# A decoder block's expert layer: the last quarter of the experts computed densely on TensorE beside the gathers of the rest

## What is computed

```python
q = (h @ w_peer_q).reshape(b, s, 8, 2, 128)
sc = jnp.einsum('bshcd,hckd->bshck', q, peer_keys)
s1, i1 = lax.top_k(sc[..., 0, :], 16)
s2, i2 = lax.top_k(sc[..., 1, :], 16)
cand_s = s1[..., :, None] + s2[..., None, :]
cand_i = i1[..., :, None] * 128 + i2[..., None, :]
top_s, pos = lax.top_k(cand_s, 16)        # of the 256 pairs
eid = take_along_axis(cand_i, pos)
gate = softmax(top_s)
act = gelu(einsum('bthkd,btd->bthk', peer_u[eid], h))
out = x + einsum('bthk,bthkd->btd', gate * act, peer_v[eid])
```

## Time and profile before

| | |
|---|---|
| median of 3 runs | 2677.69 us |
| the profiled execution, its time | 2674.36 us |
| its span (first to last instruction) | 2672.7 us |
| mean granted TensorE clock | 0.811 of full |
| busy: TensorE, VectorE, ScalarE, GpSimd | 1696.7, 1703.4, 780.6, 710.3 us |
| bytes read from HBM | 771 MB, of which the gathers' queue 549 MB |

### The profile page before, as it was taken

How to read it: one execution, slowest core, us unless ns; L and a number is a source line. 1 busy time by engine, 2 the same in 40 slices (tenths; PEclk the granted TensorE clock), 3 DMA queues, 4 the chain that set the end, 5 groups by cost and what they waited for, 6 DMA issues and landing times.

```text
span 2672.7 us, 29348 instructions
## 1 busy us (share of the span) xinstructions
PE 1696.7 (63%) x9753; PEld 1263.9 (47%) x9753; DVE 1703.4 (64%) x2813; ACT 780.6 (29%) x1250; POOL 710.3 (27%) x617
## 2 busy tenths in 40 slices
PE   7899999999999999999850223223223222322335
PEld 6798888888888988878850000000000000000001
DVE  5888637766766766775787566665666665665530
ACT  4456445545554554545330000000000000000000
POOL 1000001001001001040125554435544435444332
PEclk9799999999999999999985665665666666656667
DMA  5244555665556556565778999999999999999998
GB/s 181 85 150 134 177 178 182 196 188 181 169 191 196 164 189 197 164 227 182 259 260 342 420 420 420 420 420 419 417 419 418 414 421 415 420 416 420 420 380 317
DMA packets 210987, 774.25 MB, mean 290 GB/s; under 512 B 18920, under 2 KB 54112, under 8 KB 143456
## 3 DMA queue, kind: packets, MB, share of 16 engines
q0 software_dynamic: 75584, 549.49, 50.2%
q1 hardware_dynamic: 134832, 223.61, 26.4%
q10 hardware_dynamic: 496, 0.23, 0.0%
HBM read 771.09 MB, written 2.16 MB: 289 GB/s over the span
## 4 chain that ended last, share of the span: by engine, by line
PE 43%; DMA 29%; DVE 15%; issue 7%; POOL 4%; ACT 1%; DVEq 0%; POOLq 0%; ACTq 0%; SPq 0%
DMA u_slots<-in_peer_u_dram,eid 26%; DVE u_slots L1386 6%; PE accA L1514 5%; PE accA L1516 5%; PE accA L1515 5%; PE accB L1514 4%; PE accB L1516 4%; PE accB L1515 4%; DMA v_slots<-in_peer_v_dram,v_eid 3%; DVE weight L1402 2%; POOL v_slots L631 2%; PE accB L1507 2%; PE accB L1506 2%; PE accB L1508 2%; POOL u_slots L621 2%
## 5 line engine op out<-in xcount | busy, mean ns | idle before, releaser
L1386 DVE CUSTOM_DVE_ANT_0 u_slots<-u_slots,h 128x2048 f32<-128x2048 f32 x256 | 584.1, 2291 | 431.5 <-DMA u_slots<-in_peer_u_dram,eid 428.4
L975 DVE TENSOR_TENSOR w_lo<-w_raw,w_hi 128x1024 fp32r<-128x1024 f32 (+1 forms) x420 | 523.2, 1256 | 287.4 <-ACT w_hi L664 285.8
L664 ACT ACTIVATE w_hi<-w_raw 128x1024 fp32r<-128x1024 f32 (+1 forms) x420 | 442.2, 1057 | 427.0 <-PE accB L1516 139.3
L621 POOL DMA_INDIRECT u_slots<-in_peer_u_dram,eid x256 | 310.9, 1214 | 730.3 <-DVE dots L1386 528.3
L1841 PE MATMUL accA<-v_slots,weight 128*32 128x512 f32 x512 | 114.8, 1046 | 523.7 <-DMA v_slots<-in_peer_v_dram,v_eid 523.7
L1841 PE MATMUL small<-v_slots,weight 128*32 128x512 f32 x512 | 115.4, 1051 | 387.8 <-DMA v_slots<-in_peer_v_dram,v_eid 387.8
L631 POOL DMA_INDIRECT v_slots<-in_peer_v_dram,v_eid x256 | 298.4, 1165 | 134.2 <-issue 78.8
L1841 PEld LDWEIGHTS accA<-v_slots,weight 128*32 128x32 f32 x512 | 21.8, 158 | 592.8 <-issue 592.8
L1841 PEld LDWEIGHTS small<-v_slots,weight 128*32 128x32 f32 x512 | 21.9, 158 | 457.5 <-issue 457.5
L918 ACT ACTIVATE gate<-pair_v,g_max 128x16 f32<-128x16 f32 x16 | 4.9, 308 | 533.9 <-DVE g_max L1359 533.8
L1506 PE MATMUL accB<-act_hi,w_hi 128*128 128x256 f32 x512 | 145.1, 283 | 1.9 <-ACT ya L830 1.1
(11 more groups left out here) (363 smaller groups left out, 3832.2 us busy)
## 6 DMA issues: line engine op xcount, KB each, us to landing
w_raw<-in_w_in_dram SPq DMA_DIRECT2D x168, 512.0 KB, 3.5
w_raw<-in_w_in_dram SPq DMA_DIRECT2D x128, 256.0 KB, 3.0
w_raw<-in_w_o_ssm_dram SPq DMA_DIRECT2D x64, 512.0 KB, 4.1
w_raw<-in_w_o_attn_dram SPq DMA_DIRECT2D x32, 512.0 KB, 4.4
w_raw<-in_w_out_dram SPq DMA_DIRECT2D x32, 512.0 KB, 4.6
...
```

What stands on the lines that cost most here:

```text
L621: pool.indirect_dma_start(u_slots[:, n % U_RING, :], None, peer_u[0], bass.IndirectOffsetOnAxis(ap=eid[:, u, k:k + 1], axis=0)).then_inc(u ...
L664: act.activation(w_hi[:, slot, :, 0:w], w_raw[:, slot, :, 0:w], ACT.Copy).then_inc(hi_split, 1)
L975: dve.tensor_tensor(w_lo[:, slot, :, 0:w], w_raw[:, slot, :, 0:w], w_hi[:, slot, :, 0:w].bitcast(F32), ALU.subtract).then_inc(lo_split, 1)
L1386: dve.tensor_tensor_reduce(slot, slot, h2[:, u // PH, :], 1.0, 0.0, ALU.mult, ALU.add, dots[:, u, k:k + 1]).then_inc(u_free, 1)
```

## The change

A row of experts with one first key is a **block**: 128 experts, 1 MB of `peer_u` and 1 MB of `peer_v`, contiguous. The blocks of the last 32 first keys (experts from 12288 on) are now computed for all 256 tokens, picked or not, and the gathers leave out the rows of those experts.

- **The gathers** get a bound on the index: a row whose expert number is above 12287 is not fetched. The first four of u and the first eight of v fetch all rows, since their slots hold no numbers yet. `LEAD` is now counted in picks: 20.
- **Dense u.** SyncE loads a block of `peer_u` (`ud`, two buffers). TensorE turns it in four quarters of four 128x128 transposes (`turn_quarter`), ScalarE copies each to `ut`, and TensorE multiplies it with the turned `h2_t` (four matmuls of 256 columns, `dense_quarters`). ScalarE's GELU puts the block's 128 x 256 numbers into `dense` (`take_block`). 28 of the 128 quarters run ahead of unit 0, the others before the v quarters of units 0 to 5.
- **Gates of the dense experts.** In units 6 and 7, in 16 lots of 16 tokens: ScalarE writes one-hot second keys (`second_keys`: 16 squares, one ReLU), VectorE the one-hot first keys times the gate (`first_keys`), TensorE multiplies the two for each token (`scatter_gates`), and VectorE multiplies `dense` by the result (`gate_lot`).
- **Dense v.** In units 8 to 15 SyncE loads blocks of `peer_v` (`vd`, four buffers) and TensorE multiplies them with `dense` (`dense_halves`: a half is a block for 128 tokens, four matmuls of 512 columns), into the same accumulators.
- **Residual.** `push_x1` adds it by eight matmuls with the identity; ScalarE and VectorE copy the sums out at the end.
- **Selections** are made of two heads at a time, two of units 2 and 3 beside unit 0, four beside unit 1, then two beside each of units 2 to 5 (`top_units`), none after.
- **Shares.** ScalarE spreads gates and GELUs in 32 small copies (`unit_gelu`), so that the weights are one instruction of VectorE. A dense expert's gate is set to zero there (`mask_gate`).
- **Dots** write their products to a buffer of bytes (`junk`) instead of in place.

```diff
+        LEAD = PK + 4
+
+        FIRST_DENSE = NK - DENSE
+        LAST_GATHERED = FIRST_DENSE * NK - 1
...
+        EARLY_QUARTERS = 28
+        DENSE_UNITS = 6
+        LOTS = T // LOT
...
+        def top_units(u):
+
+            return (range(4), range(4, 8), range(8, 10), range(10, 12), range(12, 14), range(14, 16))[u] if u < 6 else range(0)
...
+        def quarters_before(u, q):
+
+            if u < 4:
+                n = 3 * DENSE - EARLY_QUARTERS
+                i = 4 * u + q
...
+            return DENSE // 8
...
+        def halves_before(i):
+
+            return 2 * DENSE * min(i + 1, 29) // 29 - 2 * DENSE * min(i, 29) // 29
...
+            sp.wait_ge(w_used, n_all)
+            for b in range(DENSE):
+                if b >= 2:
+                    sp.wait_ge(ut_full, 4 * (b - 1))
+                sp.dma_start(ud[:, b % 2, :], peer_u[0, (FIRST_DENSE + b) * NK:(FIRST_DENSE + b + 1) * NK, :]
+                             ).then_inc(ud_landed[b % 2], 16)
...
+                    sp.wait_ge(x1_pushed, NT)
+                elif b >= 4:
+                    sp.wait_ge(vd_free, b - 3)
+                sp.dma_start(vd[b % 4][:, :], peer_v[0, (FIRST_DENSE + b) * NK:(FIRST_DENSE + b + 1) * NK, :]
...
+                                        bass.IndirectOffsetOnAxis(ap=eid[:, u, k:k + 1], axis=0),
+                                        bounds_check=LAST_GATHERED if n >= U_RING else NK * NK - 1, oob_is_err=False
                                         ).then_inc(u_landed[n % U_RING], 16)
...
-                    gather_u(u, k)
+            def next_u(n):
+                if n % PK == 0:
+                    pool.wait_ge(unit_ids, n // PK + 1)
+                gather_u(n // PK, n % PK)
+
+            for n in range(LEAD):
+                next_u(n)
 
...
+            for n in range(PK * UNITS):
+                if n + LEAD < PK * UNITS:
+                    next_u(n + LEAD)
+                if n % PK == 0:
+                    pool.wait_ge(v_ids, n // PK + 1)
+                gather_v(n // PK, n % PK)
...
+            def take_quarter(i):
+                act.wait_ge(ut_full, i + 1)
+                if i >= 2:
+                    act.wait_ge(ut_used, i - 1)
+                act.activation(ut[:, i % 2, :, :].rearrange("p c e -> p (c e)"), small[:, i % 2, :],
+                               ACT.Copy).then_inc(ut_done, 1)
...
+                act.activation(dense[b // (DENSE // 4)][:, b % (DENSE // 4), :],
+                               pair_d[:, b % 2, 0:T], ACT.Gelu).then_inc(d_taken, 1)
...
+            def unit_gelu(u):
+
+                act.wait_ge(normed, u + 1)
+                if u >= 2:
+                    act.wait_ge(weighed, u - 1)
+                for lanes, tokens, g, picks in spread_blocks():
+                    act.activation(gm_s[lanes, u % 2, :, g], gm[tokens, u % 4, picks], ACT.Copy)
                 act.wait_ge(u_free, PK * (u + 1))
-                act.activation(gelu[:, u, :], dots[:, u, :], ACT.Gelu).then_inc(gelued, 1)
+                for lanes, tokens, g, picks in spread_blocks():
+                    ins = act.activation(gelu_s[lanes, u % 2, :, g], dots[tokens, u % 2, picks], ACT.Gelu)
+                ins.then_inc(gelued, 1)
+                for v in top_units(u):
+                    if v >= 2:
+                        unit_softmax(v)
+                        spread_ids(v)
...
+                if j >= 2:
+                    act.wait_ge(g_full, j - 1)
+                for i in range(LOT):
+                    ins = act.activation(one_second[j % 2][:, i, :], iota[:, :], ACT.Square,
+                                         bias=picks_t[:, 2, j * LOT + i:j * LOT + i + 1])
+                ins.then_inc(squares, 1)
+                act.wait_ge(squares, j + 1)
+                act.activation(one_second[j % 2][:, :, :], one_second[j % 2][:, :, :], ACT.Relu, scale=-1.0,
+                               bias=iota[:, 1:2]).then_inc(second_ready, 1)
...
+            take_quarter(0)
+            take_quarters(EARLY_QUARTERS)
+            unit_gelu(0)
+            for u in range(PH):
+                if u == DENSE_UNITS:
+                    for r in range(4):
...
+                for q in range(4):
+                    if u < DENSE_UNITS:
+                        take_quarters(quarters_before(u, q))
+                    elif u < DENSE_UNITS + 2:
+                        for j in range(2):
+                            second_keys(8 * (u - DENSE_UNITS) + 2 * q + j)
+                    if q == 3:
+                        unit_gelu(u + 1)
...
                     i = PK * u + k
                     dve.wait_ge(u_landed[i % U_RING], (i // U_RING + 1) * 16)
+                    if i >= 2:
+                        dve.wait_ge(u_free, i - 1)
...
+                    dve.tensor_tensor_reduce(junk[min(u, 1)][:, i % 2, :], slot,
+                                             h2[:, 0, :] if u < PH else h2_late[:, :], 1.0, 0.0, ALU.mult, ALU.add,
+                                             dots[:, u % 2, k:k + 1]).then_inc(u_free, 1)
...
             def weights_of(u):
 
-                dve.wait_ge(gate_exp, u + 1)
-                step(dve.reciprocal(g_inv[:, 0:1], g_sum[:, u:u + 1]))
                 dve.wait_ge(gelued, u + 1)
...
-                dve.wait_ge(shared, u + 1)
+                dve.tensor_tensor(share_s[:, u % 2, :, :], gelu_s[:, u % 2, :, :], gm_s[:, u % 2, :, :],
+                                  ALU.mult).then_inc(shared, 1)
...
-                for g in range(4):
-                    tokens = slice(g * GROUP, (g + 1) * GROUP)
-                    for i in range(4):
...
-                            weight[i * GROUP:(i + 1) * GROUP, u % 2, :, g, :],
-                            ident[tokens, tokens].unsqueeze(1).broadcast_to([GROUP, 4, GROUP]),
-                            share[tokens, u, 4 * i:4 * i + 4].unsqueeze(2).broadcast_to([GROUP, 4, GROUP]), ALU.mult)
-                ins.then_inc(weighed, 1)
...
+                dve.wait_ge(shared, u + 1)
+                dve.tensor_tensor(weight[:, u % 2, :, :, :].rearrange("p q g i -> p (q g) i"),
+                                  block_ident[:, :].unsqueeze(1).broadcast_to([P, PK, GROUP]),
+                                  share_s[:, u % 2, :, :].rearrange("p q g -> p (q g)").unsqueeze(2)
+                                  .broadcast_to([P, PK, GROUP]), ALU.mult).then_inc(weighed, 1)
...
+                o = one_first[:, j % 2, :, :]
...
+                step(dve.tensor_tensor(o, iota[:, FIRST_DENSE:NK].unsqueeze(1).broadcast_to([P, LOT, DENSE]),
+                                       picks_t[:, 0, lot].unsqueeze(2).broadcast_to([P, LOT, DENSE]), ALU.is_equal))
+                dve.tensor_tensor(o, o, picks_t[:, 1, lot].unsqueeze(2).broadcast_to([P, LOT, DENSE]),
+                                  ALU.mult).then_inc(first_ready, 1)
...
+                dve.wait_ge(g_full, j + 1)
+                gates = small[:, j % 2, :].rearrange("p (t b) -> p b t", b=DENSE)
+                n = DENSE // 4
+                for i in range(4):
+                    o = dense[i][:, :, j * LOT:(j + 1) * LOT]
+                    ins = dve.tensor_tensor(o, o, gates[:, i * n:(i + 1) * n, :], ALU.mult)
+                ins.then_inc(g_taken, 1)
...
+            def turn_quarter(i):
+                b, q = i // 4, i % 4
...
+                for c in range(4):
+                    k = 4 * q + c
+                    ins = transpose_to(small[:, i % 2, c * P:(c + 1) * P], ud[:, b % 2, k * P:(k + 1) * P])
+                ins.then_inc(ut_full, 1)
...
+            def dense_quarters(n):
+                for i in range(quartered[0], quartered[0] + n):
+                    b, q = i // 4, i % 4
+                    if i + 1 < QUARTERS:
+                        turn_quarter(i + 1)
+                    pe.wait_ge(ut_done, i + 1)
+                    if q == 0 and b >= 2:
+                        pe.wait_ge(d_taken, b - 1)
+                    for c in range(4):
+                        ins = pe.matmul(pair_d[:, b % 2, 0:T], ut[:, i % 2, c, :], h2_t[:, 4 * q + c, :],
+                                        start=q == 0 and c == 0, stop=q == 3 and c == 3)
+                    ins.then_inc(ut_used, 1)
+                quartered[0] += n
...
+            def scatter_gates(j):
+
...
+                for i in range(LOT):
+                    ins = pe.matmul(small[:, j % 2, i * DENSE:(i + 1) * DENSE], one_second[j % 2][:, i, :],
+                                    one_first[:, j % 2, i, :], start=True, stop=True)
+                ins.then_inc(g_full, 1)
...
+                    if t == 0:
...
+                        ins = pe.matmul(((A, B), (small, pair_d))[t][c // 2][:, c % 2, :],
+                                        dense[b // (DENSE // 4)][:, b % (DENSE // 4), t * P:(t + 1) * P],
+                                        vd[b % 4][:, c * BANK:(c + 1) * BANK], start=False, stop=t == 0 and b == DENSE - 1)
+                    if t == 1:
```

(17 more changed lines are left out.)

465 lines of the change are left out of this document (335 added, 130 removed).

## The result

The change makes the kernel slower. Its median is 2712.91 us (2710.11 to 2714.75, 4 runs) against 2676.70 us of the kernel before beside it (2674.51 to 2679.12, 4 runs): a ratio of 1.0137, 95% interval 1.0122 to 1.0152. Forecast were 2625 us, 0.70 for faster, and a range up to 2740: the time lies in the range, the direction does not.

What follows compares the result with a forecast made beforehand. The prediction took DMA bytes to bound the PEER layer: 1470 + 1037 = 2507, plus 45 + 20 + 28 + 20, gives 2620 us of span and 2625 us as median, 2.0% faster; range 2540 to 2740.

Steps and rivals of the forecast that it cites:

- Bytes: Gathers fetch 0.741 of their rows but for the first 12; their queue carries about 401 MB; 164 us less DMA.
- The start: TensorE reaches unit 0 after 28 early quarters; at 1470 us, 1037 us of DMA are outstanding; first `v_slots` matmul about 1480.
- Uneven rows: In the gathers, random gaps leave one of 16 DMA engines last: 45 us taken, between 0 and 135.
- The order around `unit_gelu`: Units 0 to 5: TensorE's quarters and VectorE's weights wait for ScalarE's copies and selections: 28 us, between 0 and 60.
- Units 6 and 7: ScalarE's 135 us for lots and related work against 119 us of gathers: 20 us taken, between 0 and 40.
- The end: Last data take 12 us, as before, and the v-only stretch of 20 gathers costs 8: 20 us in all.
- sums costed at nothing: Work of TensorE, VectorE and SyncE, and the dots' byte output, taken as covered by the DMA: 0 us.
- waits eat up just the gain: Whole kernel: waits use up just the gain; chance 0.06, of which 0.05 within 0.2% of no change.
- A: Rival for the whole kernel: all of it overlaps, even engines, no stall: 2532 us; chance 0.13.
- B: Rival: VectorE and GpSimd become one serial resource, 4.7 us a pair of gathers: 2764 us, slower; chance 0.15.
- C: Rival: TensorE's clock stays at the lower level, so its quarters take longer: 2827 us; chance 0.05.
- D: Rival: a row left out of a gather saves no DMA time: 2891 us; chance 0.04.

Runs made afterwards that it cites:

- e6: The changed kernel with 8 dense quarters ahead of unit 0 instead of 28, the other 20 spread over units 0 to 3: 2689.99 us, ratio 1.0063.
- e4: The kernel before with only the bound on the gathers' index, experts from 12288 on left out, nothing dense: 2497.21 us, one run.
- e7: The kernel before with a bound of 4095 on the gathers' index (23.9% of rows stay), nothing dense, dots writing to bytes: 2415.43 us, one run.
- e1: The changed kernel with `scale_gates` and `mask_gate` later on VectorE, half a selection or, in unit 6, four dots: 2689.50 us, ratio 1.0056.
- e2: The changed kernel with the quarters of blocks 7 to 23 over units 0 to 4 and the last 32 quarters in unit 5: 2705.55 us, ratio 1.0112.
- e8: The changed kernel with the edits of e1, e2, e5 and e6 together: 2608.15 us, ratio 0.9749 to the kernel before.
- e3: The changed kernel without the lots and the waits for them, dense experts summed without their gates: 2648.98 us, one run.
- e9: The changed kernel with dots over 1024 of the 2048 columns only: 2681.28 us, one run.
- e5: The changed kernel with `gate_lot` and `first_keys` two places (three dots) later on VectorE, nothing left out: 2670.08 us, ratio 0.9986.
- e12: The kernel of e8 with 2 dense quarters ahead of unit 0 instead of 8: 2618.11 us, ratio 0.9783.

## Why the prediction was wrong

- **Bytes, right.** The page's 413 MB, less the 12.6 that the queue carried before beside its gathers (549.5 less's 536.9), are the 401 that were forecast. The queue carries 384 MB for the 493 gathers after 1400, where 0.741 of the rows and eight whole gathers make 385. What was outstanding at 1470 was 437 MB or 1045 us; the text had 1037.
- **The start, right in time, not in worth.** The first matmul on `v_slots` came at 1478.0 (about 1480 forecast). But the DMA ran at 210 GB/s from 1385 to 1470, where the earlier trace rows had 298 and more. I wrote down that the queue would stop at 24 and 4 gathers and took it as given; e6 shows that the order of the 28 quarters costs 20 us.
- **"Uneven rows", 45 us: near in size by luck, wrong in cause.** 62 us are lost by a busy DMA. By e4 and e7 the cause is the price of the rows left out, not one engine's fuller list: 484 gathers at e4's 0.13 us are 63, at e7's price of a row 40. The sum had put that price at nothing.
- **"The order around `unit_gelu`", 28 us: the step that failed first.** 56 us of idle DMA in units 0 to 5. I had ScalarE's 7 and 4 us and who waits for the weights. I had not asked what is queued on VectorE behind a wait that the change adds: `scale_gates` waits for ScalarE's softmax, dots stand behind it, and GpSimd behind the dots. The four slots of u do not hide it (e1: 22 us). And I had not looked at what `dense[3]` lies on (e2: 7 us alone). These two explain about half of the 56; e8, with both mended, still has 32 us of idle DMA from 1470 to 1930 (460 us at 0.93).
- **"Units 6 and 7", 20 us: the step that failed most.** 48 us of idle DMA and 64 by e3. I weighed ScalarE's 135 us of work against 119 us of gathers, work against work. The runs showed a closed chain over four engines in its place, with a gather's landing time in it, and moving the lots by three dots, with no work less, gave back 40.
- **The end, 20 us.** 25 to 31 with the last 110 us. Near enough.
- **The sum.** 45 + 28 + 20 + 20 = 113 us of losses became 195. Forecast: 1470 + 1037 + 113 = 2620 us of span. Measured: 1470 + 1045 + 195 = 2710. The case nearest to it, that waits eat up just the gain, had 0.06, and the time went 1.4% past that. I had a slower side only for other mechanisms. One of the sums costed at nothing has a slip that changes nothing: the dots from 1440 to 2560 are 511 us of VectorE, not 504, which leaves 7.6 us for a selection, not 8.1.
- **The signs.** The 401 MB, the start near 1480 and the mean issue under 1.5 us (1.47) came as forecast. The rate of 400 GB/s from 1400 on did not, nor the clock above 0.85: it was 0.82 from 1385 to 2710. The last sign came true, which said that with the bytes as counted and the end above 2672 the waits were mis-sized.
- **The rivals.** A (all overlaps) fell: 2532 is 76 us below even e8. B's mechanism is real and its price was too high (4.7 us a pair, 4.0 measured), and e9 shows that it does not decide. C: the clock was 0.84 in units 0 to 5 and 0.66 only in the lots' stretch, and TensorE was busy 352 of 505 and 118 of 185 us, so not full. It has a small part in the lots' chain: its quarter there took 5.6 us start to start, 3.6 in unit 4 at 1851 us. No run tests these 2 us a turn apart. D: a row left out is not free, but an eighth to a fifth of a row. The Trainium skill, DMA: Bandwidth & Descriptors, "The descriptor swizzle", which fixes the engine by the partition, could not be weighed: the share leaves no more than 1% for its consequence here, and no run shows the dealing itself.

What stays open: the rest of the idle DMA in units 0 to 5, whether the 24 us that e5 leaves of e3's 64 are the lots' work or what is left of the chain, e12's 10 us, and whether a third order of ScalarE's `unit_gelu` would take the 20.4 us that VectorE still waits at unit 6 in e8. They were not tried.
